# A mixer's gate scans and an expert unit's last low part, put elsewhere in the engines' queues

## The reference

```python
def hybrid_mixer(x, ...):
    r_q, r_k, r_v, r_g, c_q, c_kv, k_r, m_q, m_k, m_v, m_o, m_i, m_f = split(x @ w_in)
    ret = retention(rope(r_q), rope(r_k), r_v)               # 4 heads
    qf = rms_norm(c_q) @ w_uq;  kvf = rms_norm(c_kv) @ w_ukv
    att = mla_attention(q_nope, rope(q_rope), k_nope, rope(k_r), v)   # 8 heads, softmax
    qk = silu(causal_dwconv(concat(m_q, m_k), conv_w, conv_b))        # 4 taps
    hcell = mlstm(mq, mk, m_v, m_i + b_i, m_f + b_f)         # 4 heads; cumulated gates
    return concat(..ret.., att, ..hcell..) @ w_out

def moe_swiglu(x, ...):
    for e in range(8):
        y += gate[:, e] * ((silu(x @ wg[e]) * (x @ wu[e])) @ wd[e])   # inner width 3584
```

## Time and profile before

| what | value |
|---|---|
| median of three runs | 2418.15 us (2417.14 to 2418.49) |
| the profiled execution's own time | 2416.57 us |
| its span, first to last instruction | 2415.0 us |
| TensorE busy | 2323.7 us, 96% of the span |
| VectorE busy | 1867.5 us, 77% |
| ScalarE busy | 1421.8 us, 59% |
| DMA | 615.89 MB, mean 255 GB/s |

### The profile page before, as it was taken

The page is one execution under the profiler, slowest core; times in us unless marked ns, Lnnn a source line. Parts: engine busy times, 40 slices in busy tenths (PEclk is TensorE's granted clock), DMA queues, the critical chain, the costliest instruction groups (busy, mean ns, idle before and its releaser), DMA issues.

```text
span 2415.0 us, 35278 instructions
## 1 busy us (share of the span) xinstructions
PE 2323.7 (96%) x13084; PEld 1998.6 (83%) x13084; DVE 1867.5 (77%) x2136; ACT 1421.8 (59%) x1434; POOL 65.9 (3%) x80
## 2 busy tenths in 40 slices
PE   9999999999999998989989979999999999999994
PEld 8877999897789998789978768888888888888883
DVE  5677898756779987665466769898989888889896
ACT  5565544456654436534436537777777777777773
POOL 0100000000000000000000010000000000000000
PEclk9999999999999999989999989999999999999997
DMA  6345555434465455268544349999999999999996
GB/s 252 134 151 181 213 178 189 175 141 148 149 221 188 184 192 196 72 218 259 191 157 157 140 184 397 373 381 375 381 376 377 377 380 376 378 378 375 379 376 253
DMA packets 94146, 615.89 MB, mean 255 GB/s; under 512 B 9808, under 2 KB 17632, under 8 KB 22496
## 3 DMA queue, kind: packets, MB, share of 16 engines
q1 hardware_dynamic: 88544, 591.51, 65.1%
q0 software_dynamic: 5504, 23.04, 2.5%
HBM read 599.30 MB, written 15.20 MB: 254 GB/s over the span
## 4 chain that ended last, share of the span: by engine, by line
PE 74%; issue 10%; DVE 7%; DVEq 3%; ACT 3%; DMA 1%; POOL 1%; ACTq 0%; POOLq 0%; SPq 0%
PE bank L321 23%; PE bank L323 23%; PE bank L322 23%; DVE w_lo L610 3%; DVEq L602 2%; ACT w_hi L522 1%; PE bank L392 1%; DMA raw<-in_weights_dram 1%; PE bank L469 1%; PE bank L1842 1%; PE bank L439 1%; PE bank L421 0%; PE bank L429 0%; DVE probs L669 0%; ACT probs L563 0%
## 5 line engine op out<-in xcount | busy, mean ns | idle before, releaser
L610 DVE TENSOR_TENSOR w_lo<-raw,w_hi 128x2048 fp32r<-128x2048 f32 x551 | 1250.0, 2295 | 275.4 <-ACT w_hi L522 249.8
L522 ACT CAST w_hi<-raw 128x2048 fp32r<-128x2048 f32 x552 | 1044.6, 1912 | 203.5 <-DMA raw<-in_weights_dram 196.8
L321 PE MATMUL bank<-w_hi,hT_hi 128*128 128x512 f32 (+3 forms) x1296 | 509.7, 393 | 1.9 <-DVEq L2545 1.7
L323 PE MATMUL bank<-w_hi,hT_lo 128*128 128x512 f32 (+3 forms) x1296 | 500.5, 386 | 0.0
L322 PE MATMUL bank<-w_lo,hT_hi 128*128 128x512 f32 (+3 forms) x1296 | 499.6, 385 | 0.0
L321 PE MATMUL bank<-hT_hi,w_hi 128*128 128x256 f32 x1536 | 443.6, 289 | 3.8 <-DVEq L631 1.9
L323 PE MATMUL bank<-hT_hi,w_lo 128*128 128x256 f32 x1536 | 439.0, 286 | 0.0
L322 PE MATMUL bank<-hT_lo,w_hi 128*128 128x256 f32 x1536 | 439.0, 286 | 0.0
L321 PE MATMUL bank<-w_hi,oT_hi 128*128 128x512 f32 x940 | 372.1, 396 | 6.6 <-DVE oT_lo L2558 6.3
L322 PE MATMUL bank<-w_lo,oT_hi 128*128 128x512 f32 x940 | 367.0, 390 | 0.0
L323 PE MATMUL bank<-w_hi,oT_lo 128*128 128x512 f32 x940 | 366.9, 390 | 0.0
(11 more groups left out here) (288 smaller groups left out, 1582.3 us busy)
## 6 DMA issues: line engine op xcount, KB each, us to landing
raw<-in_weights_dram SPq DMA_DIRECT2D x554, 1024.0 KB, 4.8
token_rows<-all_cols SPq DMA_DIRECT2D x11, 512.0 KB, 9.8
arena<-in_norms_dram POOLq DMA_DIRECT2D x4, 1024.0 KB, 9.0
nat<-token_rows POOLq DMA_DIRECT2D x8, 512.0 KB, 7.6
unit_rows<-probs POOLq DMA_DIRECT2D x8, 512.0 KB, 4.6
arena<-in_b_gate_dram POOLq DMA_DIRECT2D x6, 512.0 KB, 4.0
unit_rows<-all_cols SPq DMA_DIRECT2D x4, 512.0 KB, 9.4
tables<-in_tables_b_dram POOLq DMA_DIRECT2D x1, 1216.0 KB, 5.5
```

Source lines behind the costliest of these rows:

```text
L321: mm(out, st[0], mv[0], start=start, stop=False, skip_group_check=True)
L323: return mm(out, st[1], mv[0], start=False, stop=stop, skip_group_check=True)
L522: self.isa.copy(m.w_hi[:, slot, :], m.raw[:, slot, :]).then_inc(m.hi_ready, 1)
L610: self.isa.tensor_tensor(m.w_lo[:, slot, :], m.raw[:, slot, :], m.w_hi[:, slot, :].bitcast(F32), ALU.subtract).then_inc(m.lo_ready, 1)
```

## The change

In the mixers, PE's `turn_scans` moves from ahead of `rotate(QR)` to behind `latent_heads`, and one of the two value-projection parts ahead of the first `turn_probs` moves behind (the loop takes the eighth part at its own end). ACT copies head 0's turned probabilities before the second pair's exponentials. DVE ropes QR right after two splits; the first `divided` comes before the second `subtrahends`, the scans stand behind that, and the first convolution moves from behind the first pair's maxima to behind the last pair's. The copy of the turned scans moves to the end of the heads. In the experts, DVE makes the last hidden rows' low part ahead of one split rather than behind it.

```diff
@@ TensorB.mixer @@
         two_tiles(5)
-        self.turn_scans(4, ident)
         self.rotate(b_tile(m, QR, 2), 6, rot32, 2)
         self.latent_heads(ident)
+        self.turn_scans(4, ident)
         self.states(ident)
@@ TensorB.latent_heads @@
         pair(2)
         next(filler)
-        next(filler)
         self.turn_probs(0, 6, ident)
@@ ScalarB.mixer @@
         self.conv_rows_out(7, 1)
+        self.probs_out(0, 6)
         self.exp_pair(1, False)
-        self.probs_out(0, 6)
         self.probs_out(1, 6)
@@ VectorB.mixer @@
         self.roped(4, RK, 2, cos64, sin64)
-        self.split(1)
-        self.scans()
-        self.split(1)
-        self.roped(6, QR, 2, cos32, sin32)
-        (wait to_dve[4], copy to small, drain: cols_turned)
+        self.split(2)
+        self.roped(6, QR, 2, cos32, sin32)
         self.subtrahends(0, blocks, scale)
-        self.convolved(0, MQ, par)
         self.divided(0)
         self.subtrahends(1, blocks, scale)
+        self.scans()
         self.divided(1)
         self.subtrahends(2, blocks, scale)
         self.split(1)
         self.oT_low(0, 2, (7, 7))
         self.divided(2)
         self.subtrahends(3, blocks, scale)
+        self.convolved(0, MQ, par)
         self.oT_low(1, 2, (7, 7))
         self.divided(3)
         self.split(1)
         self.oT_low(2, 2, (7, 7))
         self.oT_low(3, 2, (7, 7))
         self.eng.drain().then_inc(m.oT_ready, 1)
+        (wait to_dve[4], copy to small, drain: cols_turned)
@@ VectorB.experts @@
             self.hidden_rows()
             self.gathered()
-            self.split(1)
             self.hidden_turned(LAST_HIDDEN)
-            self.split(3)
+            self.split(4)
```

More of the change, by code:

```diff
@@ L2151, in mixer @@
         self.roped(4, RK, 2, cos64, sin64)
-        self.split(1)
-        self.scans()
-        self.split(1)
+        self.split(2)
         self.roped(6, QR, 2, cos32, sin32)
-        self.eng.wait_ge(m.to_dve[4], w.next(m.to_dve[4]))
-        self.isa.tensor_copy(m.small[:, AT:AT + 16], m.bank[4][:, 0:16]).then_inc(m.free[4], 1)
-        self.eng.drain().then_inc(m.cols_turned, 1)
         blocks, scale = m.tab(B_TABLES, "blocks"), (DH + 32) ** -0.5
         self.subtrahends(0, blocks, scale)
-        self.convolved(0, MQ, par)
         self.divided(0)
         self.subtrahends(1, blocks, scale)
+        self.scans()
         self.divided(1)
@@ L2176, in mixer @@
         self.eng.drain().then_inc(m.oT_ready, 1)
+        self.eng.wait_ge(m.to_dve[4], w.next(m.to_dve[4]))
+        self.isa.tensor_copy(m.small[:, AT:AT + 16], m.bank[4][:, 0:16]).then_inc(m.free[4], 1)
+        self.eng.drain().then_inc(m.cols_turned, 1)
         self.convolved(1, MK, par)
```

## The result

| | before | after |
|---|---|---|
| median of six runs each | 2418.32 us | 2403.89 us (2401.93 to 2411.32) |
| the profiled execution's own time | 2416.57 us | 2404.63 us |
| ratio | | 0.9943, 95% interval 0.9933 to 0.9953 |

The kernel is 0.6% faster; 2403.5 was forecast. Two later measurements of the same kernel gave 0.9963 and 0.9954, so its total is known to some 5 us only, and the useful question is which terms of the predicted sum were real.

What follows compares the result with a forecast made beforehand. PE, busy for 96% of the span, was taken as the bound. Mixers 7.2 us plus experts 7.5 us made 14.7 us less, for a median of 2403.5 us; the range was 2399 to 2409.5 us.

Steps and rivals of the forecast that it cites:

- Experts, 8 x 0.94 = 7.5 us: Each experts unit: low part ahead of split removes PE's 0.94 us loss at chunk 40; eight units, 7.5 us.
- The lead of three and chunk 41 as the held split: Experts: DVE's splits run three chunks ahead of PE, so the held split is chunk 41, with 1.5 us to spare.
- Transfers cost nothing: Experts: shorter units need 381 GB/s instead of 378; a row shows 442, so this was costed at nothing.
- rival A: Experts: transfers hold the stage, so only the mixers pay, 7.2 us less, 2411.0 us; chance 0.05.
- `pair(0)` 2.6 us earlier: Each mixer: with the scans' wait gone, `pair(0)` starts 2.6 us earlier, behind a new 1.5 us wait for roped QR.
- Head 0's wait, 1.57 and 1.94 us: Mixers: PE's waits of 1.47 and 1.84 us for ACT's copy go, plus 0.10 refill: 1.57 and 1.94 us.
- The value part moved, "no gain, no loss": Mixers: the value part taken from ahead of the first turning is done at the loop's end, at no gain or loss.
- Head 6 late by 0.4: Each mixer: convolution ahead of `oT_low(1)` and `divided(3)` makes head 6 late, -0.4 us, bounds 0 and -0.8.
- Clock, one new stretch of 1.7 us: Mixers: the new 1.5 us waits bring one half-clock stretch of two possible, -1.7 us; bounds 0 and -3.4.
- The sum: First mixer 5.1, second 3.8, new half-clock stretch -1.7: mixers 7.2, experts 7.5, together 14.7 us, giving 2403.5 us.
- Rival B: Mixers: scans and convolution moved into the heads make PE stand another 3.5 us per mixer, 2410.5 us; chance 0.13.
- rival C: Experts: DVE's lead is one chunk, not three, so each unit loses 3.2 us, 2436 us in all; chance 0.02.

Runs made afterwards that it cites:

- the crossed lead runs: Kernel before with DVE's lead in the experts cut from three chunks to two: 2416.02 us; the same plus the low part ahead of the split: 2428.87 us.
- The copy alone: Kernel before with one line moved: ACT copies head 0's turned probabilities ahead of the second pair's exponentials; 2414.17 us, ratio 0.9980.

## Why the prediction was right, step by step

- **Experts, 8 x 0.94 = 7.5 us: right.** 118.60 for 119.50 in the units, 7.6 us in the experts of the kernel with this part alone; 6.6 us in the profiled execution of after, where its first unit has waits of 0.94, 0.38 and 0.19 us. The low part ends 1.26 us ahead, for 1.2 forecast. The lead of three and chunk 41 as the held split were right, and the crossed lead runs show that the sign hangs on them.
- **Transfers cost nothing: right.** 380 GB/s over the window of a unit. By the rule of the Trainium skill (DMA: Bandwidth & Descriptors, "Where 436 GB/s comes from"), about 358, this unit could not be as short as it is. The trace goes against it as a bound for this kernel, and rival A falls. The section gets the figure as half of what a stack gives to two cores, and here one core runs.
- **`pair(0)` 2.6 us earlier: right, a little low.** Measured from the norm's first matmul it starts at 47.36 for 50.30 (968.55 - 918.25) in the first mixer and 48.05 for 51.15 in the second: 2.9 and 3.1. The new wait was forecast as 1.5 and is 1.33 and 1.34.
- **Head 0's wait, 1.57 and 1.94 us: right in size, wrong in one of its two causes.** The copy alone gains 3.8 us at full clock for the 3.5 forecast. Only ACT's queue was a cause. The convolution did not have to move for this wait, and where it was put it is the cause of the wait at line 469, two points below.
- **The value part moved, "no gain, no loss": wrong.** A term of 0.66 us in each mixer was put at nothing. It is a gain, that of the last weighing: 1.49 us before and 0.83 after. No run moves the value part alone, but all nine profiles with the mixers' part have 0.81 to 0.83 here in both mixers, and all five without it 1.49.
- **Head 6 late by 0.4: wrong wait, and twice the size.** PE has no wait for head 6's probabilities. It waits at bank 7, for `oT_low(1)` behind the convolution: 0.89 and 0.85 us, and 0.1 for the refill, beyond the bound of 0.8. The prediction asked what the convolution does to the division behind it, and passed over the low part in front of that division, which frees a bank.
- **Clock, one new stretch of 1.7 us: mis-sized.** In this profile both new waits ahead of line 1643 have one, of 3.4 us each: 6.8 us and not 1.7, and above the bound of 3.4. In all, the mixers' half-clock part went from 10.6 to 14.8 us (13.4 and 11.7 in the other profiles). By the steps of the prediction it had to fall by 3.4: the stretch at 984 goes for the new one, and the two stretches behind the scans' waits, 1.7 us each, go within the 2.6.
- **The sum: partly luck.** In the mixers 7.2 us were forecast, of which 3.8 at full clock (7.2 less the 3.4 above). Measured are 5.1 at full clock, but only 1.0, 2.1 and 3.8 in all in three profiles. In the profiled execution the dense part made up for what was missing, with 3.7 us of clock that no edit touches. So 2403.5 against 2403.89 is closer than its terms were, and that is luck. Of the two later medians one is 2403.90, and one is 2409.85, just over the range.
- Rival B (waits in the heads) was real in kind, with 0.87 in place of 3.5 us in each mixer; rival C is right as a mechanism, but was priced too low: it had the change turn slower only with a lead of one, and a lead of two cost 0.45 us a unit. With a lead of two the experts' edit costs 1.6 us a unit, 12.9 us in all (2428.87 - 2416.02). That is more than the 5.1 us of the mixers, so with that lead the whole change would have been slower (an estimate; no run has both).

What stays open: what decides whether a wait is followed by a half-clock stretch that costs nothing, 1.7 or 3.4 us.

## What to carry to other kernels

When a wait is taken away, look at what PE meets next within 2 us: here the rope behind a split cost 1.34 us of idle time and 1.7 to 3.4 us of clock in each mixer. When work is moved past others in a queue, go through everything that it now stands ahead of, instructions that only give back a buffer or bank too. Whether an activation's low part should go ahead of a weight split depends on which chunk that split is for: count the lead first. And compare the time of the matmuls themselves, not only the idle pieces: a pair of heads of which one was not ready cost 0.66 us without any bracket.

## What the runs showed of the hardware

**A short wait and the clock.** Behind the wait of 1.34 us ahead of line 1643 the granted clock fell to 0.50 in ten of ten cases (five profiles, two mixers), for 1.7 us of loss in three and 3.4 in seven. In the four profiles without this wait it stayed at 1.00 there in eight of eight. Behind 1.91 us ahead of line 1621 the loss was 1.7 us in ten of ten. Behind 1.47 and 1.84 us ahead of line 439 it was 0 (two), 1.7 (one) or 3.4 us (five). So a wait's length does not set the price: 1.34 us cost as much as 1.91 us or twice that. At line 439 one and the same wait cost nothing in one profile and 3.4 us in another. The Trainium skill (TensorE: Matmul & The Clock Gate, "What's actually happening") has the gate follow how busy PE was recently. The rows agree in that the price does not follow from the wait alone, and they don't show more.

**Two heads side by side.** A weighing has eight matmuls, four for each of two heads, each with 64 output rows. With both heads' probabilities there, the matmuls of the two heads start 13 or 14 ns apart (1323.22 and 1323.24 in the kernel after), and all eight take 0.81 to 0.83 us at full clock. With the second head's copy not yet done they come head after head and take 1.49 us (ten of ten last weighings with the mixers of before).

**Executions of one kernel differ by their clock.** The 20 executions of the kernel after go from 2401.6 to 2413.4 us, in groups that go with their mean granted clock over the execution: 2401.6 to 2403.1 at 0.981 or 0.982, 2403.6 to 2404.6 at 0.980, 2406.6 and 2407.0 at 0.978 and 0.979, and 2409.9 to 2413.4 at 0.977. From 0.977 to 0.982 is 0.005 of 2400 us, 12 us, which is the whole spread (an estimate from these numbers). The medians of its three measurements, of six, five and nine executions, each fall in one of the groups: 2403.89, 2409.85 and 2403.90. That fits the ratios of 0.9943, 0.9963 and 0.9954, though the runs of the kernel before differ between the measurements too.
